# Hybrid trunk on one core: a seventh of the ten input-projection units is multiplied in fp32r parts in both mixers

## The reference, cut to what matters

```python
for i in range(DEPTH):                                   # DEPTH = 2
    u = rms_norm(h, attn_norm_g[i]) @ w_in[i]            # 256 tokens x 1024 @ 1024 x IN_COLS
    u_conv, z, xbc, dt_raw, c_q, c_kv, k_rope = split_in(u)
    y_conv = conformer_conv(u_conv, ...)                 # 31-tap depthwise conv, group norm, silu
    y_ssd = ssd_mixer(z, xbc, dt_raw, ...)               # 4-tap depthwise conv + silu on xbc, then SSD
    y_mla = mla_mixer(c_q, c_kv, k_rope, ...)            # latent attention, 4 heads
    h = h + jnp.concatenate([y_conv, y_ssd, y_mla], axis=-1) @ w_out[i]
    hn = rms_norm(h, ffn_norm_g[i])
    h = h + (swiglu(hn, ...) if i % 2 == 0 else moe_top2(hn, ...))
    h = h + (p[i] @ ple_w_proj[i]) * sigmoid(rms_norm(h, ple_norm_g[i]) @ ple_w_gate[i])
return rms_norm(h, final_norm_g)
```

## Time and profile before

| | us |
|---|---|
| median of 3 runs | 1429.22 |
| the profiled execution, device time | 1428.27 |
| its span, first to last instruction | 1426.5 |
| TensorE busy / weight loads busy | 1387.9 / 1004.9 |
| DVE busy | 854.5 |
| ACT busy | 697.4 |

### The profile page before, as it was taken

How to read it: one execution, slowest core, us unless ns; L and a number is a source line. 1 busy time by engine, 2 the same in 40 slices (tenths; PEclk the granted TensorE clock), 3 DMA queues, 4 the chain that set the end, 5 groups by cost and what they waited for, 6 DMA issues and landing times.

```text
span 1426.5 us, 18333 instructions
## 1 busy us (share of the span) xinstructions
PE 1387.9 (97%) x7015; PEld 1004.9 (70%) x7015; DVE 854.5 (60%) x988; ACT 697.4 (49%) x785; POOL 6.9 (0%) x14
## 2 busy tenths in 40 slices
PE   6999999999999999999999999999999999999997
PEld 6877888888887788766666666666666766666635
DVE  6997636463479978746454656455555455555426
ACT  6566534442555657544444444444444453544316
POOL 0000000000000000000000000000000000000000
PEclk9999999999999999999999999999999999999998
DMA  9425565555544009999999999999999999999992
GB/s 334 158 66 172 178 191 190 180 182 201 167 150 146 8 5 417 421 419 419 420 413 420 419 418 420 414 416 419 418 419 419 415 415 419 418 420 419 419 410 92
DMA packets 99670, 443.89 MB, mean 311 GB/s; under 512 B 7729, under 2 KB 22097, under 8 KB 99329
## 3 DMA queue, kind: packets, MB, share of 16 engines
q1 hardware_dynamic: 98688, 439.30, 78.5%
q0 software_dynamic: 896, 3.44, 0.7%
HBM read 440.61 MB, written 2.10 MB: 310 GB/s over the span
## 4 chain that ended last, share of the span: by engine, by line
PE 84%; DMA 6%; DVE 6%; ACT 2%; issue 1%; ACTq 0%; DVEq 0%; SPq 0%
PE psum L642 19%; PE psum L643 18%; PE psum L644 18%; PE psum L1176 11%; PE psum L1190 7%; DMA ring<-in_moe_w_up 4%; DMA ring<-in_moe_w_down 2%; PE psum L693 2%; PE psum L1080 1%; PE psum L711 1%; ACT w_hi L1506 1%; PE psum L1205 1%; DVE arena_a L2105 1%; DVE ring_lo L2018 1%; PE psum L665 1%
## 5 line engine op out<-in xcount | busy, mean ns | idle before, releaser
L2018 DVE TENSOR_TENSOR ring_lo<-ring,w_hi 128x1792 fp32r<-128x1792 f32 x191 | 384.3, 2023 | 278.8 <-ACT w_hi L1506 277.3
L1506 ACT ACTIVATE w_hi<-ring 128x1792 fp32r<-128x1792 f32 x191 | 323.8, 1700 | 286.4 <-DMA ring<-in_moe_w_down 119.0
L644 PE MATMUL psum<-w_hi,hidden_b 128*128 128x512 f32 x624 | 229.6, 368 | 0.0
L2012 DVE TENSOR_TENSOR ring_lo<-ring,w_hi 128x2048 fp32r<-128x2048 f32 (+1 forms) x68 | 152.6, 2265 | 101.4 <-ACT w_hi L1500 101.4
L1176 PE MATMUL psum<-ring,xT 128*64 128x512 f32 (+1 forms) x1024 | 201.7, 543 | 0.0
L642 PE MATMUL psum<-w_hi,hidden_b 128*128 128x512 f32 (+1 forms) x512 | 190.3, 372 | 1.9 <-DVE ring_lo L2018 1.8
L643 PE MATMUL psum<-ring_lo,hidden_b 128*128 128x512 f32 (+1 forms) x512 | 187.1, 365 | 0.0
L642 PE MATMUL psum<-w_hi,xT_parts 128*128 128x512 f32 (+1 forms) x384 | 150.0, 391 | 1.9 <-DVE ring_lo L2012 1.8
L1176 PEld LDWEIGHTS psum<-ring,xT 128*64 128x64 f32 x1024 | 69.8, 137 | 114.1 <-issue 112.0
L642 PE MATMUL psum<-w_hi,hidden_a 128*128 128x512 f32 (+1 forms) x384 | 146.7, 382 | 2.7 <-DVE ring_lo L2018 2.7
L644 PE MATMUL psum<-w_hi,xT_parts 128*128 128x512 f32 (+1 forms) x384 | 148.6, 387 | 0.0
(11 more groups left out here) (338 smaller groups left out, 1453.8 us busy)
## 6 DMA issues: line engine op xcount, KB each, us to landing
ring<-in_moe_w_gate SPq DMA_DIRECT2D x128, 896.0 KB, 8.9
ring<-in_moe_w_up SPq DMA_DIRECT2D x128, 896.0 KB, 9.8
ring<-in_moe_w_down SPq DMA_DIRECT2D x128, 896.0 KB, 9.5
ring<-in_w_in SPq DMA_DIRECT2D x16, 1024.0 KB, 6.0
ring<-in_dense_w_gate SPq DMA_DIRECT2D x14, 1024.0 KB, 5.1
ring<-in_dense_w_up SPq DMA_DIRECT2D x14, 1024.0 KB, 5.1
ring<-in_dense_w_down SPq DMA_DIRECT2D x14, 1024.0 KB, 4.9
ring<-in_w_out SPq DMA_DIRECT2D x8, 1024.0 KB, 5.1
```

The costliest lines, as they stand in the source:

```text
L644: return mm(o, a[1], b[0], start=False, stop=final)
L1506: A(heavy_high(c), moe_raw(m), ACT.Copy).then_inc(hi_ready, 1)
L2012: V.tensor_tensor(low(g, sizes[g]), raw(g, sizes[g]), f32(high(g, sizes[g])), ALU.subtract).then_inc(lo_ready, 1)
L2018: V.tensor_tensor(moe_low(m), moe_raw(m), f32(heavy_high(c)), ALU.subtract).then_inc(lo_ready, 1)
```

## The change

Unit 6 leaves `RAW_IN`. It is now split on ACT and DVE and multiplied in parts by TensorE in both layers; units 7, 8 and 9 stay exact. Two `split(f + 6)` calls are added, one in ACT's `mixers`, behind the logarithm of dt, and one in DVE's, ahead of convolution taps 8 to 12. Since two more units of the program are parted, the rotating `w_hi` slots that later parted units use move on by one or two places.

```diff
-RAW_IN = (6, 7, 8, 9)
+RAW_IN = (7, 8, 9)
...
                 act.wait_ge(dtu_ready, L + 1)
                 A(dtl, dtu, ACT.Ln).then_inc(dtl_ready, 1)
+                split(f + 6)
                 take_xbc(1)
                 take_xbc(2)
...
                 V.tensor_scalar(dtu, dte, 1.0, None, ALU.add).then_inc(dtu_ready, 1)
                 dve.wait_ge(dtu_ready, L + 1)
+                split(f + 6)
                 conv_taps(8, 13)
                 xbc_taps(0)
                 conv_taps(13, 17)
```

## The result

With the change the kernel takes **1451.26 us** (median of 4 runs, 1450.53 to 1451.83) against 1428.45 us (4 runs, 1427.25 to 1430.36) in the same comparison: ratio 1.0154, 95% interval 1.0141 to 1.0166. It is 1.5% slower, and the forecast was 1451.

What follows compares the result with a forecast made beforehand. DVE was taken to bound the mixers: delays of 11.14 and 11.12 us, 22.3 together, on 1428.27 make 1450.5; with the runs' median 0.95 above that execution, 1451 us. The 8-in-10 range was 1444 to 1457 us.

Steps and rivals of the forecast that it cites:

- DVE waits for the rounding: Ahead of DVE's subtraction for unit 6, layer 0: DVE idles from 44.44 to 53.68 us, 9.24 us.
- DVE's taps later: Convolution taps behind the subtraction start later by wait plus 2.20 us of work: 11.44 us in layer 0, 11.61 in layer 1.
- TensorE idle ahead of unit 6: TensorE reaches unit 6 at 49.11 us but may start only after DVE's subtraction, at 55.97 us: some 6.9 us idle.
- unit 6 in parts: 48 matmuls in parts instead of 16 plain ones: 5.75 us against 6.91, up to 7.4 us if the clock fell.
- TensorE's second wait: At L804 TensorE waits some 3.5 us for ACT's last silus, held back by DVE's last xbc taps.
- the clock: Lower TensorE clock after idling at unit 6: 0 to 1.65 us, taken as 1.65, costing the sum nothing.
- the whole, against the profiled execution: Both mixers' delays passed on in full: 11.14 + 11.12 = 22.3 us on top of 1428.27 us.
- DVE sets the end: In the mixers, DVE's lateness passes to the end, less its earlier waits of 0.30 us (layer 0) and 0.49 us (layer 1).
- the change of sides in the chain: Layer 0's chain of waits runs through TensorE to about 77 us, then through DVE until the first output-projection matmul at 108.55.
- the 6.6 us: By the skill's clock rule, two cold starts in each mixer: up to 6.6 us more if all showed at the end.
- the rival of the clock showing at the end: Cold starts at TensorE's waits not hidden, each mixer losing 1.65 us once or twice: 1454 to 1457 us, 12 in 100.
- The faster rival: TensorE bounds and operands are ready at unit 6 (49.11 us), saving 1.16 us per mixer: 1426 us, 3 in 100.

Runs made afterwards that it cites:

- the late DVE: Kernel before, with one added wait holding DVE ahead of taps 8 to 12 until ACT's logarithm: 1444.03 us, ratio 1.0111.
- the placement without waits: Changed kernel with ACT's rounding moved behind the taking of xbc 0 and DVE's subtraction behind taps 8 and 9: 1431.96 us, ratio 1.0024.
- The late TensorE: Kernel before, unit 6 still exact, with one added wait holding TensorE ahead of unit 6 until DVE has the decay inputs: 1448.61 us, ratio 1.0138.
- the seven idle matmuls: Changed kernel with 7 matmuls whose result nothing reads added on TensorE ahead of unit 6: 1450.91 us, ratio 1.015.
- fourteen idle matmuls: Changed kernel with 14 matmuls whose result nothing reads added on TensorE ahead of unit 6: 1450.42 us, ratio 1.0152.
- the subtraction later: Changed kernel with DVE's subtraction moved behind taps 8 to 16 and the first xbc taps, ACT's rounding left in place: 1447.61 us, ratio 1.0127.

## Why the prediction was right

| step | predicted | after |
|---|---|---|
| DVE waits for the rounding, layer 0 | 9.24 | 9.25 |
| DVE's taps later, layer 0 | 11.44 | 11.42 |
| the same, layer 1 | 11.61 | 11.65 |
| TensorE idle ahead of unit 6 | 6.9 | 6.80 |
| unit 6 in parts, layer 0 | 5.75 to 7.4 | 7.56 |
| the same, layer 1 | 5.75 to 7.4 | 7.31 |
| TensorE's second wait | 3.5, or 1.8 with the clock, at L804 | 2.39, at L796 |
| first output-projection matmul | 119.7 | 119.53 |
| the whole, against the profiled execution | 22.3 | 22.15 |

For layer 1, the delay that it inherits is taken off: there the taps start at 457.18 instead of 433.36 us, 23.82 us later, and its opening transposes at 413.79 instead of 401.62, 12.17 later.

The totals agree better than their parts, and that is luck. At the first matmul behind the mixer the delay is 10.98 us in layer 0 (11.14 predicted) and 10.89 us in layer 1 (498.47 and 521.53 us, less 12.17; 11.12 predicted), 21.9 us together. The rest of the 22.15 comes from outside the mixers: 0.2 us are lost again before layer 1 begins, and 0.5 us are added behind its mixer; what adds them, no run shows. One reason for the smaller parts: DVE had a second small wait for TensorE (77.10 us, 0.27 us behind the step before it; 0.08 after), which took up another 0.19 us and which the prediction did not count.

- **DVE sets the end.** That the page's busiest engine is not the one that decides was read from the change of sides in the chain and the small waits of DVE at it. That a delay of DVE beyond those waits passes on, the late DVE alone showed, and the placement without waits showed that its 2.20 us of work count by themselves. The late TensorE adds what the prediction only implied: before the change it is TensorE that comes last where the chain changes sides, by 0.30 us, so a TensorE that is later still sets the end just as well. Here it was late by 6.8 + 7.56 - 6.91 = 7.5 us, less than DVE's 11.4, so its own delay showed nowhere.
- **The order of the calls.** Nearly all came from where ACT's call stands, behind a wait for TensorE's own transposes, which come right ahead of the unit to be multiplied. Moving it gave back 15.6 of the 22.8 us.
- **Undersized: the clock.** "bound its cost on TensorE by 0 and 1.65 us and take 1.65" fell short in layer 0: it was 1.81 us, over the bound taken from the earlier trace rows, and 1.56 us in layer 1. That the bound came so near is luck, as no row shows that the 1.65 us of the earlier trace rows are the clock's: the granted clock in that opening, 10.81 to 16.30 us, reads 1.00. That the cost at unit 6 lies beside other work held, with the seven idle matmuls as the test. The Trainium skill, TensorE: Matmul & The Clock Gate, "Part 1: The HAM clock gate", has the clock fall to half when the engine pauses: the trace agrees, with 0.50 behind the wait. Of the 6.6 us that it would have added at the end, about 0.15 us are seen, in layer 0, as follows.
- **Off in place: the second wait.** It is not "at L804" but one step earlier, at the second half of L796. That writes the bank that holds the transposed q until ACT takes it out (L1638), and in ACT's order this stands right behind the silus. Same cause, DVE's last taps. The chain of waits of after, layer 0, passes there:

```profile
86.95 0.91 ACT arena_a L1620 x2
88.40 0.95 PE psum L796 x4
89.34 1.71 PE psum L804 x8
91.48 1.23 PE psum L818 x8
92.73 0.70 DVE arena_b L2221
```

So the cold TensorE has taken the lead over DVE, but only just. Two steps of DVE at that place, first before, then after:

```profile
79.75 0.69 DVE L2213 TENSOR_TENSOR arena_b<-psum,par 128x512 f32<-128x512 f32 x1
80.36 0.68 DVE L2219 SCALAR_TENSOR_TENSOR arena_b<-psum,par 128x512 f32<-128x512 f32 x1
...
91.97 0.69 DVE L2215 TENSOR_TENSOR arena_b<-psum,par 128x512 f32<-128x512 f32 x1
92.73 0.69 DVE L2221 SCALAR_TENSOR_TENSOR arena_b<-psum,par 128x512 f32<-128x512 f32 x1
```

From the one to the other DVE takes 0.61 us before and 0.76 after, where it waits for the scores of L818; with fourteen idle matmuls, which keep TensorE from pausing there, it is 0.61 us again (90.92 to 91.53). In layer 1 of after it is 0.61 us too, and nothing is lost. So the rival of the clock showing at the end had the mechanism, but at about 0.15 us once instead of 1.65 us once or twice in each layer; the 0.73 us in the kernel with seven show that it could have been more.

The faster rival fell at its own condition: with the rounding in ACT's gap and operands in time the kernel was still 0.24% slower than before, because the work moved from TensorE, in part, to DVE. No version tried beats the kernel before.

## What to carry to other kernels

Before work is traded from one engine to another, ask which of the two is late where their chains meet, not which has the higher busy share over the whole kernel: 1.16 us off TensorE were paid with 2.20 us on DVE, at a place where TensorE came last by only 0.30 and 0.49 us, so that DVE's added work had no more room than that. A helper step for a multiplication belongs ahead of the wait on the producer that runs just before that multiplication; put behind it on an in-order engine, it stops two engines at once. And of two engines' delays take the larger, not the sum.

## What the runs showed that was not expected

- The price of a pause on TensorE's clock varies. After 6.80 us idle the 48 matmuls in parts lost 1.81 us in layer 0 and 1.56 us in layer 1 of the same execution; after 8.48 us idle, with the subtraction later, they lost 2.48 us (59.05 to 67.28); after 7.55 us idle the plain fp32 unit lost 3.1 us (9.99 against 6.91). So the length of the pause and the work behind it do not set the price alone; what else does, no run here shows.
- At the start of the program the same 32 transposes took 5.49 us in one execution and 6.59 us in the other, which is 1.1 us of difference that no edit made. The granted clock reads 1.00 in both, so the cause stays open.
- A subtraction on an idle GpSimd all but stopped DVE's two-input taps: 4.18 us lost in 4.58 us.
